# Two-layer streaming encoder: MLP evictions set between the squares at the layer's inner crossing, and the mixed queries of two attention heads kept on one bank

## The chip, the cores and the metric

One core of a Trainium2 chip runs the whole kernel in one launch. The metric is device time in microseconds, the median of several runs of the same program; lower is better.

## The reference, cut to what matters

The model is two layers on 560 tokens (512 frames, 16 meta tokens, 32 sample tokens), width 1024. Each layer mixes tokens in three branches, merges them, and ends in a squared-ReLU MLP:

```python
h = _rmsnorm(x, p['g_pre_mix'])
... = _split_cols(h @ p['w_in'])
oa = ...   # latent attention A, 8 heads, chunk-causal
x = x + _rmsnorm(mix, p['g_post_mix'])
f = jnp.square(jax.nn.relu(_rmsnorm(x, p['g_pre_mlp']) @ p['w_ff1'])) @ p['w_ff2']
return x + _rmsnorm(f, p['g_post_mlp'])
```

In latent attention each of 8 heads has 512 frame queries and 48 others: 16 meta queries, which see 16 meta keys, and 32 sample queries, which see 256 cached keys, 16 cached meta keys and 32 new keys. The 48 are the "mixed" queries of the change; they are scored against 320 keys under a mask:

```python
s_fr = jnp.where(visible, s_fr, NEG)
prob = jax.nn.softmax(jnp.concatenate([s_meta, s_fr], axis=-1), axis=-1).astype(v.dtype)
```

## The kernel before, in words

Tokens lie along the free dimension, in two halves of 280, and channels along the partitions. A dense projection is cut into units of 1024x128 weights. Each weight tile is loaded by SyncE into `wraw`, split by ScalarE into a rounded part `whi`, and by VectorE or GpSimd into the rest `wlo`. Each activation tile is split in the same way (`h_hi`, `h_lo`). For each of 8 k-tiles TensorE then does three matmuls (hi by hi, hi by lo, lo by hi) with 280 moving columns, so that a half unit ("half") is 24 matmuls, and a "pair" of units, interleaved by k-tile, is 48 (L926).

All engines walk one list of steps, `plan`, written out by hand in `lap` and `layer_plan`; each engine does its part of a step and skips the rest. So the order of steps in `plan` is the order on ScalarE and VectorE as well as on TensorE. Waits are on one counter for each engine.

`lap` writes the two crossings of a layer, where TensorE would otherwise wait for a norm: "post_mix" (from the output projection to `ff1`) and "post_mlp" (from `ff2` to the next layer). While TensorE does the last six units of the one projection on the second half of the tokens and the first six units of the next on the first half, VectorE and ScalarE bring the second half of `x` through two norms. For half 1 of "post_mix" the steps are: `rstd` of the first norm; for each pair of tiles j = 0 to 3, `norm` (VectorE L1820 and L1826: scale, add to x) and `square` (ScalarE L1416, then a sum on VectorE L1800); `sums`; a matmul with ones that sums over partitions (`mean_square`, step "ms", L940); `rstd` (ScalarE L1406 and L1407); `tokens`, which makes `h_raw` (L1854), `h_hi` (L1321) and `h_lo` (L1843). The evictions of the `ff1` units on half 0, three ScalarE instructions each (L1376 ReLU from PSUM, L1387 square, L1321 rounding), stand in the same list. `free` lets the planner put weight splits at that place, `hold` forbids it.

Latent attention has 16 jobs in a layer, (t, i): two heads t and 128 frame queries i. Step ("att", "a", j) does the scores of job j on TensorE, the transposes (`turn`) of job j-1 and the product with the values (`values`) of job j-2, and is followed by a dense unit. The jobs with i = 0, four in each layer, carry the mixed queries of both heads besides: scores of 48 queries by 320 keys for each head a, into banks S0 + a (L1140), softmax on VectorE, ScalarE and GpSimd over both heads as 48 partitions by 640 columns, and four transposes for each head (L1164).

Of the kernel before, what the change touches and what calls it, by code (L numbers as in the profile page):

```python
# [142 lines left out]
def build(nc, io, known):  # L143
    st = Steps(known)
    ctx = ExitStack()
    with ctx:
# [129 lines left out]
        ptm = at("ptm", [META, 2, 256], F32, work)  # L276
        stat, _ = wt("stat", [P, 2, 24])
# [35 lines left out]
        k_spread = sem("rope_keys_spread")  # L313
        state_loaded = sem("state_loaded")
# [68 lines left out]
        def program(block):  # L383
# [50 lines left out]
            def lap(l, post, pre, first, second):  # L434
# [36 lines left out]
                for i, u in enumerate(units[2:], 2):  # L471
                    if i == LAP - 3:
                        plan.append((l, ("hold",)))
# [245 lines left out]

            PARTS = (range(0, 4), range(4, 6), range(6, KD))  # L720
# [38 lines left out]
            def prob_view(j, i):  # L759
                nk = key_count("a", i)  # L760
                c0 = 2 * key_count("a", 0) if i == 4 else 0
                return prob[j % 2][:, c0:c0 + 2 * nk].rearrange("p (a n) -> p a n", a=2)

# [6 lines left out]
            def _(sp):  # L770
# [37 lines left out]
                for l, u in list(slot_of)[LAP:]:  # L808
# [29 lines left out]
            def _(pe):  # L838
# [277 lines left out]
                def scores(br, j):  # L1116
                    _, t, i = JOBS[br][j]
                    if br == "a":
# [10 lines left out]
                        for a in range(2):  # L1129
# [9 lines left out]
                            if i == 0:  # L1139
                                mm = pe.matmul(ps[0:MIXED, S0 + a, 144:144 + K_META], q_cat[:, h, META0:T], k_cat[:, h, 0:K_META],  # L1140
                                               start=False, stop=True, skip_group_check=True)
                    mm.then_inc(pe_done, st.done("pe", f"{br} scores {j}"))

                def turn(br, j):
# [8 lines left out]
                    if br == "a":  # L1153
                        for a in range(2):
# [5 lines left out]
                            if i == 0:  # L1160
                                pm = prob_view(j, 4)
                                idn = const[0:MIXED, 0:MIXED]
                                for n_, (c0, w) in enumerate(((0, 128), (128, 128), (CKEYS, MIXED), (PAST, META))):
                                    mm = pe.transpose(ps[0:w, T0 + a, 128 + 48 * n_:176 + 48 * n_], pm[0:MIXED, a, c0:c0 + w], idn)  # L1164
                    mm.then_inc(pe_done, st.done("pe", f"{br} turn {j}"))

                def values(j):
# [16 lines left out]
                    if i == 0:  # L1184
                        dst, mixed = ps[:, M_, 0:MIXED], slice(0, MIXED)
                        tiles = [(va_c[:, 0, :], lambda a: pt_third[:, a, 0:48], mixed), (va_c[:, 1, :], lambda a: pt_third[:, a, 48:96], mixed),
                                 (va_mix[:, :], lambda a: pt_third[0:MIXED, a, 96:144], mixed),
                                 (va_cm[:, :], lambda a: pt_third[64:64 + META, a, 144:192], mixed)]
# [115 lines left out]
            def _(act):  # L1304
# [281 lines left out]
                def att(br, j):  # L1586
                    n = len(JOBS[br])
                    if j < n:
                        _, t, i = JOBS[br][j]
                        k, sc = 2, A_SCALE  # L1590
                        for tile in tiles_of(br, i):
                            act.wait_ge(dve_done, A("dve", f"{br} shift {j} {tile}"))
                            pb = prob_view(j, tile)
                            w = pb.shape[2]
                            rows = P if tile < 4 else MIXED
                            s0 = 10 if br == "a" and tile == 4 else 8
# [87 lines left out]
            def _(dve):  # L1684
# [357 lines left out]
                def att(br, j, up):  # L2042

                    n = len(JOBS[br])
                    if j < n:
# [32 lines left out]
                        if br == "a" and i == 0:  # L2078
                            pb = prob_view(j, 4)
                            rows = MIXED  # L2080
                            sm = stat[0:rows, j % 2, :]
                            ms = c_("mask_s", MIXED).rearrange("p (a n) -> p a n", a=1).to_broadcast([MIXED, 2, 320])
                            link(dve.tensor_tensor(pb[0:rows, :, :], ps[0:rows, S0:S1 + 1, 144:464], ms, ALU.add), f"a shift {j}")
# [433 lines left out]
```

## Time and profile before

| what | value |
|---|---|
| median of 3 runs | 2343.1 us (2342.99 to 2345.57) |
| the profiled execution, its own time | 2343.32 us |
| its span | 2341.6 us |
| TensorE matmul busy | 2299.3 us, 98% |
| VectorE, ScalarE, GpSimd busy | 917.3, 997.4, 935.1 us |
| granted TensorE clock, mean | 0.997 |

The span is from the first to the last instruction on the core; 1.7 us of the execution's time lie around it. Matmuls are pipelined: the time from the start of one to the start of the next is what each one costs, and the durations shown overlap. A matmul of a full float32 operand has two records, one for each pass; a float32 transpose has one.

### The profile page before, as it was taken

The numbers are of one execution on the slowest core, as the hardware profiler recorded it, in microseconds if no ns is written. First come the engines' busy times: TensorE is split into PE (matmuls) and PEld (weight loads), VectorE is DVE, ScalarE is ACT, GpSimd is POOL, SyncE is SP. The second block draws the span as 40 slices with busy tenths as digits, with TensorE's granted clock in tenths as the row PEclk, the third lists the DMA queues.
The fourth block names the chain that finished last, engine by engine and source line by source line (L and its number), as shares of the span: only waits on it lengthen the run. The fifth ranks groups of instructions, "written<-read, shape, count | busy, mean of one in ns | idle before, by whom it ended". The sixth has DMA issues, their size and how long they took to land.

```text
span 2341.6 us, 41355 instructions
## 1 busy us (share of the span) xinstructions
PE 2299.3 (98%) x17536; PEld 2173.7 (93%) x17536; DVE 917.3 (39%) x1877; ACT 997.4 (43%) x1895; POOL 935.1 (40%) x598
## 2 busy tenths in 40 slices
PE   7999999999999999999999999999999999999997
PEld 7999978889899899999999999788999999999997
DVE  6566455543514401000575664555344152000014
ACT  4444334433555642432344444334345555423312
POOL 2222224344665354544412223144455644545532
PEclk9999999999999999999999999999999999999999
DMA  5122221112224122222321223211222241222222
GB/s 193 53 66 62 87 68 57 53 59 76 64 82 149 64 89 82 90 82 72 117 88 53 71 62 97 62 55 55 64 64 67 86 166 49 88 83 90 84 81 75
DMA packets 59368, 187.71 MB, mean 80 GB/s; under 512 B 8048, under 2 KB 17104, under 8 KB 58672
## 3 DMA queue, kind: packets, MB, share of 16 engines
q1 hardware_dynamic: 50960, 169.09, 22.7%
q10 hardware_dynamic: 8224, 15.97, 1.9%
q8 instruction: 140, 2.29, 0.4%
q14 instruction: 44, 0.36, 0.0%
HBM read 170.87 MB, written 10.89 MB: 78 GB/s over the span
## 4 chain that ended last, share of the span: by engine, by line
PE 92%; DVE 5%; ACT 2%; issue 1%; POOL 0%; DMA 0%; SPq 0%; DVEq 0%; ACTq 0%
PE dense L897 43%; PE att L897 30%; PE att L972 2%; PE att L1192 1%; PE att L1112 1%; PE att L1049 1%; PE dense L926 1%; PE att L1132 1%; PE att L1230 1%; PE att L1053 1%; PE att L1035 1%; PE att L1156 1%; PE att L1265 1%; PE att L1136 1%; PE att L926 1%
## 5 line engine op out<-in xcount | busy, mean ns | idle before, releaser
L2243 POOL TENSOR_TENSOR wlo<-wraw,whi 128x1024 fp32r<-128x1024 f32 x245 | 587.8, 2406 | 592.4 <-ACT whi L1317 592.4
L897 PE MATMUL dense<-h_hi,whi 128*128 128x280 f32 x1888 | 556.6, 295 | 1.2 <-ACT hid_raw L1376 0.9
L897 PE MATMUL dense<-h_lo,whi 128*128 128x280 f32 x1888 | 550.4, 292 | 0.0
L897 PE MATMUL dense<-h_hi,wlo 128*128 128x280 f32 x1888 | 549.3, 291 | 0.0
L1317 ACT ACTIVATE whi<-wraw 128x1024 fp32r<-128x1024 f32 x302 | 314.8, 1050 | 268.4 <-DMA wraw<-in_w 266.6
L897 PEld LDWEIGHTS dense<-h_hi,whi 128*128 128x128 f32 x1888 | 355.0, 188 | 14.6 <-issue 9.4
L897 PEld LDWEIGHTS dense<-h_hi,wlo 128*128 128x128 f32 x1888 | 354.5, 188 | 0.5
L897 PEld LDWEIGHTS dense<-h_lo,whi 128*128 128x128 f32 x1888 | 354.8, 188 | 0.0
L897 PE MATMUL att<-h_hi,whi 128*128 128x280 f32 x1024 | 299.3, 292 | 0.4 <-issue 0.4
L897 PE MATMUL att<-h_lo,whi 128*128 128x280 f32 x1024 | 298.4, 291 | 0.0
L897 PE MATMUL att<-h_hi,wlo 128*128 128x280 f32 x1024 | 297.8, 291 | 0.0
L897 PE MATMUL att<-hid_hi,whi 128*128 128x280 f32 x672 | 196.0, 292 | 0.0
L897 PEld LDWEIGHTS att<-h_hi,whi 128*128 128x128 f32 x1024 | 192.4, 188 | 3.5 <-ACT sig L1340 1.6
L897 PE MATMUL att<-hid_lo,whi 128*128 128x280 f32 x672 | 195.7, 291 | 0.0
L897 PE MATMUL att<-hid_hi,wlo 128*128 128x280 f32 x672 | 195.4, 291 | 0.0
L897 PEld LDWEIGHTS att<-h_hi,wlo 128*128 128x128 f32 x1024 | 192.3, 188 | 0.3
L897 PEld LDWEIGHTS att<-h_lo,whi 128*128 128x128 f32 x1024 | 192.4, 188 | 0.0
L2248 POOL TENSOR_TENSOR hid_lo<-hid_raw,hid_hi 128x560 fp32r<-128x560 f32 (+1 forms) x76 | 91.5, 1204 | 246.5 <-ACT hid_hi L1321 246.5
L2291 POOL TENSOR_TENSOR level<-bcum 128x256 f32<-128x256 f32 (+2 forms) x56 | 40.4, 722 | 262.8 <-DVE bcum L1875 262.8
L897 PEld LDWEIGHTS att<-hid_hi,whi 128*128 128x128 f32 x672 | 126.3, 188 | 0.1
L897 PEld LDWEIGHTS att<-hid_lo,whi 128*128 128x128 f32 x672 | 126.3, 188 | 0.0
L897 PEld LDWEIGHTS att<-hid_hi,wlo 128*128 128x128 f32 x672 | 126.2, 188 | 0.1
(361 smaller groups left out, 4624.4 us busy)
## 6 DMA issues: line engine op xcount, KB each, us to landing
wraw<-in_w SPq DMA_DIRECT2D x302, 512.0 KB, 3.5
x_spill<-x ACTq DMA_DIRECT2D x2, 2240.0 KB, 6.9
x<-x_spill ACTq DMA_DIRECT2D x2, 2240.0 KB, 12.3
k_cat<-k_rope SPq DMA_DIRECT2D x16, 212.0 KB, 3.4
x<-in_x SPq DMA_DIRECT2D x4, 560.0 KB, 6.0
out_y_out<-x SPq DMA_DIRECT2D x4, 560.0 KB, 3.1
out_c_out<-ckv SPq DMA_DIRECT2D x2, 560.0 KB, 5.3
state<-in_state ACTq DMA_DIRECT2D x8, 128.0 KB, 2.1
```

The costliest lines, as they stand in the source:

```text
L897: mm = pe.matmul(bank(u, o, hf)[0:m, :], a[:, k, o * 128:o * 128 + m], b[:, k, H[hf]], start=(k == 0 and i == 0), stop=(k == kt - 1 and i ...
L926: mm = pe.matmul(bank(u, 0, hf)[0:m, :], a[:, k, 0:m], b[:, k, H[hf]], start=(k == 0 and i == 0), stop=(k == KD - 1 and i == 2))
L972: mm = pe.matmul(ps[0:rows, PAIR_BANK[i], c0:c0 + 64].rearrange("p (g t) -> p g t", t=m), e[:, 128 * sb:128 * sb + rows], late, start=(n_ ...
L1035: mm = pe.matmul(ps[:, bank, 256 * (sb % 2):256 * (sb % 2) + 256], ktok[0:n, sb, :], vtok[0:n, sb, :], start=(sb % 2 == 0), stop=True, ski ...
L1049: pe.matmul(dst, vtok[0:n, sb, 128 * vt:128 * vt + 128], amat[0:n, a:a + n], start=first, stop=(sb == 0), skip_group_check=True)
L1053: mm = pe.matmul(dst, state[:, STATE_IN[sb], 128 * vt:128 * vt + 128], qe[:, a:a + n], start=False, stop=True, skip_group_check=True)
L1112: mm = pe.matmul(ps[0:n, pair + i, 0:512], src[:, k, a:a + n], wuv[:, k, :], start=(k == 0), stop=(k == KL - 1))
L1132: mm = pe.matmul(ps[:, S0 + a, 0:META + 128 * (i + 1)], q_cat[:, h, 128 * i:128 * i + 128], k_cat[:, h, K_META:K_FRAME + 128 * (i + 1)], s ...
L1317: act.activation(whi[slot][:, :], wraw[slot][:, :], ACT.Copy).then_inc(act_done, st.done("act", f"w hi {u}"))
L2243: pool.tensor_tensor(wlo[slot][:, :], wraw[slot][:, :], whi[slot][:, :].bitcast(F32), ALU.subtract).then_inc(pool_done, st.done("pool", f" ...
L2248: pool.tensor_tensor(lo, raw, hi.bitcast(F32), ALU.subtract).then_inc(pool_done, st.done("pool", name))
L2291: pool.tensor_tensor(e_first, ref, b_first, ALU.subtract).then_inc(pool_done, st.done("pool"))
```

## The change

Two things are changed.

At the "post_mix" crossing the steps of half 1 are written in another order: the pair of the first two `ff1` units and its evictions come ahead of the second square, the third unit's half comes ahead of the third square and the fourth unit's ahead of the last. TensorE's own order is the same as before.

In the attention jobs with i = 0 the mixed queries of head 0 are given 64 columns (48, and 16 columns of the next head that nothing reads) and those of head 1 48 columns, on output partitions 0 to 63 and 64 to 111 of the one bank S0. From there on both heads are one tile of 112 partitions by 320 columns: two mask additions, one reduction, one subtraction, one exponential, one reciprocal, one multiplication, and four transposes of 112 rows in place of eight of 48. The second head's mask is a new tile, `mixed_mask`, on partitions 64 to 111, which SyncE loads in each layer behind the weights of unit up_c 1, after it has waited for the outputs that lay there (`latent_stored`).

```diff
+        mixed_mask = at("mixed_mask", [P, 320], F32, work)
...
-                crossed(1, 1)
-                plan.append((l1, ("pair", units[0:2], 0, (l, post))))
-                crossed(1, 2)
-                crossed(1, 3)
-                plan.extend([(l, ("sums", pre, 1)), (l, ("free",))])
-                plan.extend([(l1, ("after", v, 0)) for v in units[0:2]])
+                if post == "post_mix":
+                    plan.append((l1, ("pair", units[0:2], 0, (l, post))))
+                    plan.extend([(l1, ("after", v, 0)) for v in units[0:2]])
+                    plan.append((l, ("hold",)))
+                    crossed(1, 1)
+                    plan.append((l1, ("half", units[2], 0)))
+                    crossed(1, 2)
+                    plan.append((l1, ("half", units[3], 0)))
+                    crossed(1, 3)
+                    plan.extend([(l, ("sums", pre, 1)), (l, ("free",)), (l, ("hold",))])
+                else:
...
+                    if UNITS[u] == ("up_c", 1):
+                        sp.wait_ge(latent_stored, 32 * (l + 1))
+                        sp.wait_ge(pe_done, A("pe", f"gla z {C_HEADS - 1}", l))
+                        m0 = CONST["mask_s"][0]
+                        sp.dma_start(mixed_mask[64:64 + MIXED, :], io["const"][0:MIXED, m0:m0 + 320]).then_inc(mask_loaded, 16)
...
-                            if i == 0:
-                                mm = pe.matmul(ps[0:MIXED, S0 + a, 144:144 + K_META], q_cat[:, h, META0:T], k_cat[:, h, 0:K_META],
-                                               start=False, stop=True, skip_group_check=True)
+                        if i == 0:
+                            every_q = q_cat.rearrange("p h t -> p (h t)")
+                            for a, n in ((0, 64), (1, MIXED)):
+                                h = 2 * t + a
+                                mm = pe.matmul(ps[64 * a:64 * a + n, S0, 144:144 + K_META], every_q[:, h * T + META0:h * T + META0 + n],
+                                               k_cat[:, h, 0:K_META], start=False, stop=True, skip_group_check=True)
...
-                                for n_, (c0, w) in enumerate(((0, 128), (128, 128), (CKEYS, MIXED), (PAST, META))):
-                                    mm = pe.transpose(ps[0:w, T0 + a, 128 + 48 * n_:176 + 48 * n_], pm[0:MIXED, a, c0:c0 + w], idn)
+                                n = 128 + TWO_MIXED
+                                for bank_, c0, at_c, w in ((T0, 0, 128, 128), (T0, 128, n, 128), (T1, CKEYS, 128, MIXED), (T1, PAST, n, META))[2 * a:2 * a + 2]:
+                                    mm = pe.transpose(ps[0:w, bank_, at_c:at_c + TWO_MIXED], prob_mixed(j)[:, c0:c0 + w],
+                                                      const[0:TWO_MIXED, 0:TWO_MIXED])
...
+                            dve.wait_ge(mask_loaded, 16 * (l + 1))
+                            both = ps[0:rows, S0, 144:464]
+                            dve.tensor_tensor(pb[0:64, :], both[0:64, :], c_("mask_s", 64), ALU.add).then_inc(dve_done, st.done("dve"))
+                            link(dve.tensor_tensor(pb[64:rows, :], both[64:rows, :], mixed_mask[64:rows, :], ALU.add), f"a shift {j}")
+                            link(dve.tensor_reduce(sm[:, 6:7], pb[:, :], AX.X, ALU.max))
+                            dve.tensor_tensor(pb[:, :], pb[:, :], sm[:, 6:7].to_broadcast([rows, 320]), ALU.subtract
```

Line numbers of the changed kernel are higher by 31 or more at the places shown below (L1416 is L1447 in it, L1376 is L1407, L1132 is L1157).

ScalarE at the "post_mix" crossing of layer 0, before; `nsum<-x` are the squares, `hid_raw` and `hid_hi` the evictions of `ff1` units, `whi` a weight split:

```order
546 L1317 ACTIVATE whi_80<-wraw_54 128x1024
547 L1317 ACTIVATE whi_81<-wraw_55 128x1024
548 L1416 ACTIVATE nsum<-x 128x560 x4
549 L1317 ACTIVATE whi_82<-wraw_56 128x1024
550 L1376 ACTIVATE hid_raw<-dense 128x280
551 L1387 ACTIVATE hid_raw<-hid_raw 128x280
552 L1321 ACTIVATE hid_hi<-hid_raw 128x280
553 L1376 ACTIVATE hid_raw<-att 128x280
554 L1387 ACTIVATE hid_raw<-hid_raw 128x280
555 L1321 ACTIVATE hid_hi<-hid_raw 128x280
```

All four squares stand ahead of the first eviction. The same place in the changed kernel, from the first square to the last:

```order
548 L1447 ACTIVATE nsum<-x 128x560
549 L1407 ACTIVATE hid_raw<-dense 128x280
550 L1418 ACTIVATE hid_raw<-hid_raw 128x280
551 L1352 ACTIVATE hid_hi<-hid_raw 128x280
552 L1407 ACTIVATE hid_raw<-att 128x280
553 L1418 ACTIVATE hid_raw<-hid_raw 128x280
554 L1352 ACTIVATE hid_hi<-hid_raw 128x280
555 L1447 ACTIVATE nsum<-x 128x560
556 L1407 ACTIVATE hid_raw<-att 128x280
557 L1418 ACTIVATE hid_raw<-hid_raw 128x280
558 L1352 ACTIVATE hid_hi<-hid_raw 128x280
559 L1447 ACTIVATE nsum<-x 128x560
```

Two evictions now stand behind the first square, one behind the second and, in the rows that follow, one behind the third; `whi_82` comes behind the fourth square as before, and only the fifth unit's eviction is left behind the second `rstd`, where it was before too. VectorE's order at the crossing does not change.

TensorE at the transposes of the first job with i = 0 (layer 0), before; `const` is the identity:

```order
1937 L1156 MATMUL att<-const,prob_142 128x128
1938 L1158 MATMUL att<-const,prob_142 16x128
1939 L1164 MATMUL att<-const,prob_142 128x48 x2
1940 L1164 MATMUL att<-const,prob_142 48x48
1941 L1164 MATMUL att<-const,prob_142 16x48
1942 L1156 MATMUL att<-const,prob_142 128x128
1943 L1158 MATMUL att<-const,prob_142 16x128
1944 L1164 MATMUL att<-const,prob_142 128x48 x2
1945 L1164 MATMUL att<-const,prob_142 48x48
1946 L1164 MATMUL att<-const,prob_142 16x48
```

and in the changed kernel:

```order
1936 L1184 MATMUL att<-const,prob_142 128x128
1937 L1186 MATMUL att<-const,prob_142 16x128
1938 L1191 MATMUL att<-const,prob_142 128x112 x2
1939 L1184 MATMUL att<-const,prob_142 128x128
1940 L1186 MATMUL att<-const,prob_142 16x128
1941 L1191 MATMUL att<-const,prob_142 48x112
1942 L1191 MATMUL att<-const,prob_142 16x112
```

Twelve transposes have become eight. TensorE at the scores of the same job, in the changed kernel, with a row of the dense units on either side (before, the order was frames, mixed, frames, mixed):

```order
1883 L922 MATMUL dense<-oc_lo,whi_77 128x280
1884 L1157 MATMUL att<-k_cat,q_cat 128x144 x2
1885 L1168 MATMUL att<-k_cat,q_cat 64x320
1886 L1168 MATMUL att<-k_cat,q_cat 48x320
1887 L922 MATMUL dense<-h_hi,whi_75 128x280
```

The two mixed matmuls now stand side by side.

## Rows read from the trace of the kernel before

**Rows 1.** The page: busy time, share and instructions of each engine.
```profile
PE 2299.3 (98%) x17536; PEld 2173.7 (93%) x17536; DVE 917.3 (39%) x1877; ACT 997.4 (43%) x1895; POOL 935.1 (40%) x598
```

**Rows 2.** Waits of TensorE: waiter, releaser, total us, times, longest.
```profile
PE dense L926 <- DVE h_lo L1843: 7.7, 4, 3.4
```

**Rows 3.** Timeline, TensorE, crossing of layer 0: start, us, instruction, idle before.
```profile
783.56 0.74 PE L940 MATMUL att<-nsum,const 128*128 128x280 f32 x2 [0.44 <-DVE nsum L1803]
784.74 0.37 PE L897 MATMUL dense<-h_hi,whi 128*128 128x280 f32 x1 [0.45 <-ACT hid_raw L1376]
...
787.78 0.29 PE L897 MATMUL dense<-h_lo,whi 128*128 128x280 f32 x1
791.50 0.37 PE L926 MATMUL dense<-h_hi,whi 128*128 128x280 f32 x1 [3.43 <-DVE h_lo L1843]
...
799.43 0.29 PE L897 MATMUL att<-h_hi,whi 128*128 128x280 f32 x1
```

**Rows 4.** Stretches of TensorE: length, busy (matmuls), granted clock, DMA share, GB/s.
```profile
792.98:796.39 3.41, 3.41 (x16) 0.50 0.00 0
796.39:799.43 3.04, 3.04 (x25) 1.00 0.02 5
```

**Rows 5.** Timeline, ScalarE, the same crossing.
```profile
777.28 0.67 ACT L1416 ACTIVATE nsum<-x 128x560 f32<-128x560 f32 x1 [3.27 <-DVE x L1826]
...
781.57 0.67 ACT L1416 ACTIVATE nsum<-x 128x560 f32<-128x560 f32 x1 [1.47 <-DVE x L1826]
...
783.10 0.38 ACT L1376 ACTIVATE hid_raw<-dense 128x280 f32<-128x280 f32 x1
...
788.02 0.48 ACT L1406 ACTIVATE rstd<-att,const 128x280 f32<-128x280 f32 x1
```

**Rows 6.** Timeline, VectorE, the same crossing.
```profile
794.39 1.38 DVE L1843 TENSOR_TENSOR h_lo<-h_raw,h_hi 128x560 fp32r<-128x560 f32 x2
```

**Rows 7.** Timeline, TensorE, scores of an i = 0 job (its second).
```profile
387.64 0.41 PE L1132 MATMUL att<-k_cat,q_cat 128*128 128x144 f32 x2
387.98 0.74 PE L1140 MATMUL att<-k_cat,q_cat 128*48 128x320 f32 x2
388.65 0.51 PE L1132 MATMUL att<-k_cat,q_cat 128*128 128x144 f32 x2
389.09 0.74 PE L1140 MATMUL att<-k_cat,q_cat 128*48 128x320 f32 x2
389.76 0.66 PE L1156 MATMUL att<-const,prob 128*128 128x128 f32 x4
```

**Rows 8.** Timeline, TensorE, transposes of the same job, to the next matmul.
```profile
397.98 0.27 PE L1156 MATMUL att<-const,prob 128*128 128x128 f32 x1
...
398.29 0.40 PE L1164 MATMUL att<-const,prob 48*128 48x48 f32 x4
...
399.33 0.65 PE L1192 MATMUL att<-ptf,va 128*64 128x256 f32 x3
```

**Rows 9.** Timeline, TensorE, transposes of an i = 1 job, six in all.
```profile
409.20 0.38 PE L1156 MATMUL att<-const,prob 128*128 128x128 f32 x2
...
409.95 0.44 PE L1192 MATMUL att<-pt_third,va_c 128*64 128x48 f32 x8
```

**Rows 10.** Timeline, TensorE, values of branch B: two outputs, partitions 0-63 and 64-127, one bank.
```profile
588.68 0.59 PE L1265 MATMUL att<-ptf,v_own 128*64 128x512 f32 x1
588.68 0.59 PE L1265 MATMUL att<-ptf_second,v_own 128*64 128x512 f32 x1
589.11 0.59 PE L1265 MATMUL att<-ptf,v_prev 80*64 80x512 f32 x1
```

**Rows 11.** Timeline, GpSimd: the softmax multiplications of the i = 0 job.
```profile
395.24 1.87 POOL L2316 TENSOR_TENSOR prob<-prob,stat 128x288 f32<-128x288 f32 x2 [5.01 <-DVE stat L2134]
```

**Rows 12.** Timeline, SyncE's queue, from unit gate_c 1 on: start, us to the last issue.
```profile
316.45 1.04 SPq L823 DMA_DIRECT2D out_kr_out<-kra  x1
330.86 20.41 SPq L779 DMA_DIRECT2D wraw<-in_w  x2
```

More of the change, by code:

```diff
@@ L464, in lap @@
                 plan.extend([(l, ("rstd", post, 1)), (l, ("norm", post, 1, 0)), (l, ("free",)), (l, ("square", pre, 1, 0))])
-                crossed(1, 1)
-                plan.append((l1, ("pair", units[0:2], 0, (l, post))))
-                crossed(1, 2)
-                crossed(1, 3)
-                plan.extend([(l, ("sums", pre, 1)), (l, ("free",))])
-                plan.extend([(l1, ("after", v, 0)) for v in units[0:2]])
+                if post == "post_mix":
[9 more added lines that the diff above has]
+                else:
+                    crossed(1, 1)
+                    plan.append((l1, ("pair", units[0:2], 0, (l, post))))
+                    crossed(1, 2)
+                    crossed(1, 3)
+                    plan.extend([(l, ("sums", pre, 1)), (l, ("free",))])
+                    plan.extend([(l1, ("after", v, 0)) for v in units[0:2]])
                 for i, u in enumerate(units[2:], 2):
+                    if post == "post_mix" and i < 4:
+                        continue
                     if i == LAP - 3:
@@ L1185, in values, with of_head @@
                         dst, mixed = ps[:, M_, 0:MIXED], slice(0, MIXED)
-                        tiles = [(va_c[:, 0, :], lambda a: pt_third[:, a, 0:48], mixed), (va_c[:, 1, :], lambda a: pt_third[:, a, 48:96], mixed),
-                                 (va_mix[:, :], lambda a: pt_third[0:MIXED, a, 96:144], mixed),
-                                 (va_cm[:, :], lambda a: pt_third[64:64 + META, a, 144:192], mixed)]
+                        turned = pt_third.rearrange("p a n -> p (a n)")
+                        def of_head(rows, n):
+                            return lambda a: turned[rows, TWO_MIXED * n + 64 * a:TWO_MIXED * n + 64 * a + MIXED]
+                        tiles = [(va_c[:, 0, :], of_head(slice(0, P), 0), mixed), (va_c[:, 1, :], of_head(slice(0, P), 1), mixed),
+                                 (va_mix[:, :], of_head(slice(0, MIXED), 2), mixed), (va_cm[:, :], of_head(slice(64, 64 + META), 3), mixed)]
                     for n_, (v, pt, cols) in enumerate(tiles):
@@ L1592, in att @@
                             act.wait_ge(dve_done, A("dve", f"{br} shift {j} {tile}"))
+                            if tile == 4:
+                                act.activation(prob_mixed(j), prob_mixed(j), ACT.Exp, scale=sc, accum_out=stat[0:TWO_MIXED, j % 2, 10:11]
+                                               ).then_inc(act_done, st.done("act", f"{br} exp {j} {tile}"))
+                                continue
                             pb = prob_view(j, tile)
                             w = pb.shape[2]
-                            rows = P if tile < 4 else MIXED
-                            s0 = 10 if br == "a" and tile == 4 else 8
+                            rows, s0 = P, 8
                             for a in range(k):
@@ L2126, in att @@
                     if j < n:
-                        k = 2
                         i = JOBS[br][j][2]
                         for tile in tiles_of(br, i):
-                            s0 = 2 if br == "a" and tile == 4 else 0
-                            sm = stat[0:P if tile < 4 else MIXED, j % 2, :]
+                            s0, k = (2, 1) if tile == 4 else (0, 2)
+                            sm = stat[0:P if tile < 4 else TWO_MIXED, j % 2, :]
                             dve.wait_ge(act_done, A("act", f"{br} exp {j} {tile}"))
@@ L2310, in att @@
                             pool.wait_ge(dve_done, A("dve", f"{br} rsum {j} {tile}"))
[L2311 to L2316 removed]
+                            if tile == 4:
+                                pb = prob_mixed(j)
+                                rs = stat[0:TWO_MIXED, j % 2, 14:15].to_broadcast([TWO_MIXED, 320])
+                            else:
+                                pb = prob_view(j, tile)
+                                rs = stat[:, j % 2, 12:14].rearrange("p (a n) -> p a n", n=1).to_broadcast([P, k, pb.shape[2]])
+                            pool.tensor_tensor(pb, pb, rs, ALU.mult
                                                ).then_inc(pool_done, st.done("pool", f"{br} prob {j}" if tile == tiles_of(br, i)[-1] else None))
```

30 lines of the change are left out of this document (12 added, 18 removed).

## The prediction

> **What bounds the kernel now.** I read the page's busy times first: TensorE's matmuls fill 98% of the span and no other engine passes 43% [rows 1]. So a change is worth what it takes out of TensorE's row of instructions, idle time or issue time, and work saved on VectorE, ScalarE and GpSimd counts only where TensorE waits for it. The list of TensorE's waits comes next. The largest entry inside the kernel, 7.7 us in four waits, is a matmul of a pair (L926) that waits for `h_lo`; the longest is 3.4 us [rows 2]. The timeline puts one at 791.50 in layer 0 [rows 3]; layer 1 has its twin, and the other two of the four are 0.4 us each. The 791.50 matmul is the first of the pair on half 1, behind the norm that crosses from the output projection into the MLP. Then the granted clock: 1.5 us after the pair starts it falls to 0.50 for 3.41 us, the lower of its two levels (1.2 of 2.4 GHz), and TensorE gets 16 matmuls done in 3.41 us where it did 25 in the 3.04 us that followed [rows 4]. What the engine did before the fall was to stand idle for 3.43 us; after the waits of 0.4 us in the same stretch it did not fall. I charge the fall to the long wait. From the last matmul ahead of the wait, 787.78, to the first behind the pair, 799.43, 11.65 us pass [rows 3] for 48 matmuls.
>
> **Why the pair waits.** The chain is: sum of squares, matmul with ones at 783.56 [rows 3], `rstd` on ScalarE, `h_raw`, `h_hi`, `h_lo`, pair. The matmul with ones is over at 784.30 (783.56 and 0.74), but `rstd` starts at 788.02 [rows 5]. In between ScalarE does four evictions of `ff1` units, from 783.10 to 788.02, 1.23 us each. So the chain is held 3.7 us by evictions that could have been done earlier: ScalarE had idled 3.27 us ahead of the square at 777.28 and 1.47 us ahead of the one at 781.57 [rows 5].
>
> **The change, part by part. 1: the crossing.** Of those four evictions two go behind the first square, one behind the second, one behind the third. Do they fit without making a square late? TensorE does units back to back ahead of the matmul with ones, so its ends follow backwards from 783.56 - 0.44 = 783.12 [rows 3] in steps of 24 x 0.128 = 3.07 us: 780.05 for the fourth unit, 776.98 for the third, 773.9 for the pair. The first two evictions are ready at 773.9; 2 x 1.23 us bring ScalarE to 776.4, before x is ready for the square at 777.28. That square ends at 777.95, and the third eviction, whose unit is done by then, ends at 779.2, ahead of the third square, which comes 2.15 us after the second (the four are evenly spaced from 777.28 to 781.57 [rows 5]). The third square ends at 780.1, the fourth eviction at 781.4, and the last square comes at 781.57. The margins are 0.9, 0.2 and 0.2 us: thin, but a miss costs only its own amount. So the sum, and the matmul with ones, stay at 783.56, and `rstd` starts at 784.34 (in this crossing ScalarE starts 0.04 us after that matmul ends): 3.68 us earlier. All behind it moves by as much; the fifth eviction keeps its place behind `rstd`. The pair could start at 791.50 - 3.68 = 787.82, and TensorE is free at 787.78 + 0.13 = 787.91. The wait is gone, and with it, I take it, the slow clock.
>
> After it the pair needs `h_lo` at full speed. The third of its `lo` instructions, which with the fourth starts at 794.39 and takes half of 1.38 us [rows 6], ends at 791.4 when moved, and its k-tile is wanted at 791.2 (787.99 and four k-tiles of 6 x 0.128 us). I book 0.4 us for such small waits. The pair then takes 0.13 + 0.08 + 48 x 0.128 + 0.4 = 6.75 us in place of 11.65: 4.9 us. Layer 1's stretch is 0.1 us shorter, so 4.8. **Sum 9.7 us**; bounds: 10.6 without the small waits, and nothing if the squares are pushed so far that the old wait returns.
>
> **2: scores of the mixed queries.** Eight jobs in the two layers have them. Now such a job's scores take 389.76 - 387.64 = 2.12 us: for each head two frame passes of 144 columns and two mixed ones of 320. A mixed pair of passes costs 0.67 us (387.98 to 388.65) [rows 7], against 0.53 at the rate of two columns a cycle that 512 columns in 0.43 us show [rows 10]; the rest, with 0.1 us more on the frame pass ahead and 0.1 on the one behind, is the price of going from 128 output columns to 48 and back, paid twice. In the changed order the four frame passes stand together, 3 x 0.12 + 0.22, and the two mixed matmuls write partitions 0 to 63 and 64 to 111 of one bank. The trace has that form in branch B: two matmuls on halves of one bank start at the same time (588.68 both) and the next two come 0.43 us later, the time of one [rows 10]. So both heads cost what one does, 0.67. Sum 1.25, saving 0.87 us a job, **7.0 us in all**. The lower bound is that the two do not run together: 0.61 more a job, which leaves 2.1 us.
>
> **3: transposes.** Now 399.33 - 397.98 = 1.35 us for twelve [rows 8], where six of an i = 1 job, all on 128 rows, take 0.75: 0.11 each and 0.09 for the change to the 64-wide values behind them [rows 9]. A mixed group of four is cheap by its columns, but from the start of the first at 398.29 back to the next head's 128-row transpose takes 0.33 us and the way in another 0.09: the array is switched to a smaller row group and back for each head. With 112 rows I expect no switch, since matmuls on 80 rows followed those on 128 after the plain 0.43 us [rows 10]. Then eight take 4 x 0.11 + 4 x 0.096 + 0.09 = 0.91 us: 0.44 saved a job, **3.5 us in all**. If 112 rows did switch, four changes at 0.09 would leave 0.1 a job, 0.6 us.
>
> **4: the other engines.** On VectorE the mask, the reduction and the subtraction of a mixed tile fall from 640 columns to 320 (the mask in two instructions); ScalarE saves one exponential, GpSimd half of its second multiplication. None is on TensorE's path: the multiplications of job 4 end at 395.24 + 1.87 = 397.11 [rows 11], 0.87 us ahead of the transposes at 397.98 that wait for them. They get shorter, so I book nothing; what counts is that the shorter scores do not make GpSimd late, and the shorter softmax covers that. The job before loses 0.87 us of its lead (it has 1.8 us).
>
> **5: the mask's load.** SyncE now waits, behind the load of up_c 1, for `kr_out`'s landing. That store is issued at 316.45, and the load of up_c 1 is not issued before 330.86 [rows 12], when it has long landed; the mask is wanted past 353, at the first job's softmax, and is 61 KB. Booked at nothing, with some 20 us of cover.
>
> **The sum.** 9.7 + 7.0 + 3.5 = 20.2 us off the profiled execution's 2343.3, which is 0.2 above the median of 2343.1. So 2343.1 - 20.2 = **2322.9 us**.
>
> **The rivals.** (a) *The two mixed matmuls go one after the other* (chance 0.14). For it: these are 64 and 48 columns wide, not 64 and 64, and of float32 passes; against it, the pairs of rows 10. The gain is 9.7 + 2.1 + 3.5 = 15.3 us: 2327.8. The Trainium skill's page "TensorEngine Tiling (Array Packing)", under Gotcha 1: PSUM Pressure, says that different row tiles cannot access the same PSUM bank at the same time. By that rule, if it held for these two tiles, the kernel would come out at rival (a)'s time; the trace's pairs in one bank are tiles side by side in columns, and they do run together.
> (b) *112 rows are a form of their own* (0.07): 17.3 us gained, 2325.8.
> (c) *The crossing keeps its wait* (0.10). The margins of 0.2 us ahead of the third and fourth squares are eaten, or a dip of the clock stays although the wait is short. If all is kept, 10.5 us are gained: 2332.6; if half is, 2327.7.
> (d) *Slower* (0.03): the mask's load holds SyncE's queue, and with it the weight loads behind it. The next load is issued 20.4 us behind that of up_c 1 [rows 12], so a hold decides only from 20 + 10 us on in each layer (past the slack, TensorE would have to lose over 10.1 us, twice, to eat the 20.2): at 32 us, 2347. The trace speaks against it, since `kr_out` has 14 us to land before the wait is even reached.
> (e) *The change at the crossing and the concurrency as forecast, or with losses of some tenths a job in attention* (0.66): 2322.9, own range 2320.5 to 2326.
>
> **How the numbers follow.** The likeliest is (e), 2322.9. Upwards the range must take in (a), (b) and half of (c), to 2329.5; what is left out above is the full (c) and (d), about 0.1. Downwards the bound is no small waits in the pairs and transposes at the price of their columns, some 2 us more: 2320. What a measurement of this kernel can tell from no change is 0.2%, 4.7 us; every case but (d) gains more than that. Chances: faster 0.95, same 0.02, slower 0.03.
>
> **What would show it.** Part 1: no idle time ahead of the first matmul of the half-1 pair and no stretch at clock 0.50 before the end; `rstd` within 0.1 us of the end of the matmul with ones; 6.7 us from 48 matmuls. It is wrong if the squares start later against TensorE's units or the fall of the clock remains. Part 2: both mixed matmuls of a pass start within 0.01 us, and the block takes 1.25 us; if it takes 1.9, rival (a). Part 3: a block of 0.9 us; if 1.25, rival (b). Part 5: SyncE's loads at the same distance from the units.

## The result, and the profile after

The changed kernel takes 2327.1 us (median of four runs, 2326.3 to 2328.8); the kernel before, timed on the same chip, takes 2344.3. The ratio is 0.9926 with an interval of 0.9914 to 0.9938: 17.2 us faster by the medians, 16.3 by the spans of the two profiled executions (2341.6 and 2325.3). The forecast was 2322.9, a gain of 20.2; the measured time lies in the range of 2320 to 2329.5, 4.2 us above the likeliest value and above that case's own range of 2320.5 to 2326. The gain by the medians is only 3.0 us short, because the median of the kernel before has itself moved from 2343.1 to 2344.3; between the profiled executions it is 3.9 short, and that is what is explained below.

The page, where [rows 1] stood for the kernel before:

```profile
PE 2287.0 (98%) x17504; PEld 2170.0 (93%) x17504; DVE 917.2 (39%) x1885; ACT 996.0 (43%) x1879; POOL 933.9 (40%) x598
```

TensorE still sets the time. Its waits (waiter, releaser, total us, times, longest), against [rows 2]:

```profile
PE att L965 <- DVE nsum L1837: 15.4, 5, 10.9
...
PE dense L951 <- DVE h_lo L1877: 0.8, 2, 0.4
```

The wait of the pair for `h_lo` has lost its two long members: 7.7 us have become 0.8. But the first line has grown: the matmul with ones (L965, L940 before) waits for `nsum`. The same line of the list of before was

```profile
PE att L940 <- DVE nsum L1803: 12.3, 5, 10.8
```

The longest of the five is at the kernel's start in both. Of the 3.1 us more, 3.0 are in the two crossings. The timeline of TensorE at the crossing of layer 0, and behind the "..." one row of layer 1 at its end, against [rows 3]:

```profile
777.73 0.29 PE L922 MATMUL att<-h_lo,whi 128*128 128x280 f32 x1
779.96 0.74 PE L965 MATMUL att<-nsum,const 128*128 128x280 f32 x2 [1.94 <-DVE nsum L1837]
781.14 0.37 PE L922 MATMUL dense<-h_hi,whi 128*128 128x280 f32 x1 [0.44 <-issue]
...
784.20 0.29 PE L922 MATMUL dense<-h_lo,whi 128*128 128x280 f32 x1
784.32 0.31 PE L951 MATMUL dense<-h_hi,whi 128*128 128x280 f32 x1
...
791.21 0.29 PE L922 MATMUL att<-h_hi,whi 128*128 128x280 f32 x1
...
1929.69 1.30 PE L965 MATMUL att<-nsum,const 128*128 128x280 f32 x2 [1.93 <-DVE nsum L1837]
```

The pair (784.32) starts without idle time, as forecast. The matmul with ones, which had waited 0.44 us, waits 1.94. From the last matmul ahead of it, 777.73, to the first behind the pair, 791.21, are 13.48 us; the same stretch was 16.60 us before. In layer 1 it is 14.02 in place of 16.46. I call this the crossing's stretch from here on; its gain is 3.12 + 2.44 = 5.56 us, where 9.7 were forecast.

ScalarE at the same crossing, against [rows 5]:

```profile
775.28 0.68 ACT L1447 ACTIVATE nsum<-x 128x560 f32<-128x560 f32 x1 [0.24 <-DVE x L1860]
...
780.74 0.49 ACT L1437 ACTIVATE rstd<-att,const 128x280 f32<-128x280 f32 x1 [1.14 <-PE att L965]
```

The third square still finds ScalarE idle and waits 0.24 us for VectorE's `x`, and the fourth waits 0.79: the evictions fit into ScalarE, as worked out. `rstd` starts 0.04 us after the matmul with ones is over (779.96 + 0.74 = 780.70). What is late is `x`. VectorE, from the first multiplication behind the first square on (L1854 is the multiplication by `rstd`, in two instructions that are one row here, L1860 the sum into `x`):

```profile
770.39 1.46 DVE L1854 SCALAR_TENSOR_TENSOR mix<-mix,par,rstd 128x280 f32<-128x280 f32 x2
771.95 1.15 DVE L1860 TENSOR_TENSOR x<-x,mix 128x560 f32<-128x560 f32 x1
773.02 0.92 DVE L1854 SCALAR_TENSOR_TENSOR mix<-mix,par,rstd 128x280 f32<-128x280 f32 x2
...
775.17 1.47 DVE L1854 SCALAR_TENSOR_TENSOR mix<-mix,par,rstd 128x280 f32<-128x280 f32 x2
...
777.22 0.73 DVE L1860 TENSOR_TENSOR x<-x,mix 128x560 f32<-128x560 f32 x1
```

Two of the three multiplication pairs take 1.46 and 1.47 us where the middle one takes 0.92, and the first sum takes 1.15 where the last takes 0.73. The excess is 0.54 + 0.42 + 0.55 = 1.51 us, just what the matmul with ones waits longer (1.94 less 0.44). GpSimd in the same stretch:

```profile
770.23 0.89 POOL L2284 TENSOR_TENSOR hid_lo<-hid_raw,hid_hi 128x280 fp32r<-128x280 f32 x1 [27.38 <-ACT hid_hi L1352]
771.46 1.04 POOL L2284 TENSOR_TENSOR hid_lo<-hid_raw,hid_hi 128x280 fp32r<-128x280 f32 x1 [0.34 <-ACT hid_hi L1352]
775.12 0.79 POOL L2284 TENSOR_TENSOR hid_lo<-hid_raw,hid_hi 128x280 fp32r<-128x280 f32 x1 [2.62 <-ACT hid_hi L1352]
777.27 1.31 POOL L2284 TENSOR_TENSOR hid_lo<-hid_raw,hid_hi 128x280 fp32r<-128x280 f32 x1 [1.36 <-ACT hid_hi L1352]
```

Its subtractions follow each eviction (`hid_lo` is `hid_raw` less `hid_hi`), so they moved with the evictions. At 770.23, 771.46 and 775.12 they lie on the three slow steps of VectorE, and the fast one, 773.02, has none beside it. The fourth subtraction, at 777.27, shows that the order matters: VectorE's sum had begun 0.05 us earlier, at 777.22, and kept its 0.73 us, and it is the subtraction that takes 1.31 us instead of 0.79. The three slow steps of VectorE each began after the subtraction beside them. Here the one that starts second pays, and roughly what is left of the first: the sum at 771.95 began 0.55 us before the subtraction of 771.46 ended (772.50), and took 0.42 us more.

The granted clock, against [rows 4]:

```profile
1929.67:1933.08 3.41, 3.39 (x11) 0.50 0.01 2
...
780.00:783.40 3.40, 2.96 (x19) 1.00 0.00 0
```

The clock did not fall in layer 0 (1.00 behind a wait of 1.94 us), but it did in layer 1, for the same 3.41 us as before, behind a wait of 1.93 us. The prediction had named a fall that remains as a sign of being wrong.

The attention of the job of [rows 7] and [rows 8], first scores, then transposes:

```profile
386.37 0.65 PE L1157 MATMUL att<-k_cat,q_cat 128*128 128x144 f32 x4
386.95 0.75 PE L1168 MATMUL att<-k_cat,q_cat 128*64 128x320 f32 x4
387.63 0.33 PE L1184 MATMUL att<-const,prob 128*128 128x128 f32 x1
...
395.85 0.27 PE L1184 MATMUL att<-const,prob 128*128 128x128 f32 x1
396.07 0.36 PE L1191 MATMUL att<-const,prob 112*128 112x112 f32 x2
...
396.77 0.44 PE L1223 MATMUL att<-ptf,va 128*64 128x256 f32 x2
```

Scores are 387.63 - 386.37 = 1.26 us (1.25 forecast), transposes 396.77 - 395.85 = 0.92 (0.91 forecast). Summed over all jobs of both layers the score blocks went from 51.62 to 44.80 us and the transpose blocks from 33.33 to 29.55: 6.8 and 3.8, in place of 7.0 and 3.5. With the crossing's 5.6 that is 16.2 us, and the spans differ by 16.3. Nothing else of weight is in the difference.

### The profile page after: what moved, and what is told of

Same layout as the page of the kernel before. It is cut to its first block, busy times and chain, and to the rows that moved or that the text cites. A ratio compares the mean times of both kernels' runs of the same rounds, so it can differ in the third digit from the quotient of the medians.

```text
span 2325.3 us, 41287 instructions
## 1 busy us (share of the span) xinstructions
PE 2287.0 (98%) x17504; PEld 2170.0 (93%) x17504; DVE 917.2 (39%) x1885; ACT 996.0 (43%) x1879; POOL 933.9 (40%) x598
## 4 chain that ended last, share of the span: by engine, by line
PE 92%; DVE 5%; ACT 2%; issue 1%; POOL 0%; DMA 0%; SPq 0%; DVEq 0%; ACTq 0%
PE dense L922 43%; PE att L922 30%; PE att L997 2%; PE att L1223 1%; PE att L1137 1%; PE att L1074 1%; PE att L1157 1%; PE att L1261 1%; PE att L1078 1%; PE dense L951 1%; PE att L1060 1%; PE att L1296 1%; PE att L1184 1%; PE att L1161 1%; DVE x L1860 1%
```

## The experiments

The theory: *the crossing's missing 4 us come from GpSimd's subtractions, which moved with the evictions and slow VectorE's three steps ahead of the last square.* Rivals: the evictions themselves do it on ScalarE; GpSimd being busy at all does it, whatever it runs; or the shortfall lies where the two parts of the change meet.

### Each part alone

The crossing's order alone, with attention as before:

```diff
 (before, and in lap():)
+                if post == "post_mix":
+                    plan.append((l1, ("pair", units[0:2], 0, (l, post))))
+                    plan.extend([(l1, ("after", v, 0)) for v in units[0:2]])
...
```

> The kernel before with the new order at the crossing alone. Theory (the two parts add up, and GpSimd's early hid_lo subtractions hold VectorE): 5.6 us off, 0.9976 of before, and the matmul with ones waits 1.9 us as in the changed kernel. Rival (the shortfall of the changed kernel comes from the two parts together): the crossing alone gives the 9.7 us that were forecast for it, 0.9959, with a wait of 0.44 us.

Measured: 2338.9 us against 2344.6, ratio 0.9976 (0.9966 to 0.9986), span 2337.1, 4.5 us less than before. The medians give the 5.6 us that the theory expected. The matmul with ones waits 1.93 and 1.92 us, the stretches are 14.17 and 14.26 us, and the clock fell at both crossings.

Attention alone, with the old order at the crossing:

```diff
 (after, and in lap(), for post_mix too:)
+                crossed(1, 1)
+                plan.append((l1, ("pair", units[0:2], 0, (l, post))))
+                crossed(1, 2)
+                crossed(1, 3)
```

> The changed kernel with the old order at the crossing. Theory: 10.6 us off, 0.9955 of before, and at both crossings the wait of 3.4 us ahead of the pair and a fall of the clock for 3.41 us behind it. Rival (shorter attention steps make something else late): clearly under 10 us, with new waits of TensorE among the attention steps.

Measured: 2332.7 us, ratio 0.9949 (0.9934 to 0.9964), span 2330.3. The pair waits 3.43 and 3.45 us as before, the clock falls at both crossings, and no other wait is new. The spans differ by 11.3 us where 10.6 were expected. 5.7 and 11.9 us from the parts make 17.6, against 17.2 for both: the parts add up, so the shortfall is the crossing's own and is there with the old attention too.

### Moving GpSimd's subtractions away

The changed kernel with one wait more on GpSimd: the half-0 subtractions of the first six `ff1` units start only when VectorE has done its last sum into `x`.

```diff
+ if u in V_MLP and hfs == (0,):
+     pool.wait_ge(dve_done, A("dve", "x post_mix 7 1"))
```

> The changed kernel, but GpSimd begins the hid_lo subtractions of the first six ff1 units on half 0 only when VectorE has added the last tiles to x. ScalarE's evictions stay where they are. Theory (GpSimd's reads hold VectorE's two-input instructions): the three slow VectorE steps (1.46, 1.15 and 1.47 us) go back to 0.92, 0.74 and 0.92, x is ready 1.5 us earlier; the last sums and the h_raw and h_lo behind it now meet GpSimd's four subtractions and lose up to half of it again. 1 to 3 us less than the changed kernel, 0.9914 to 0.9922 of before. Rival (ScalarE's evictions hold VectorE, or the instructions are slow for their place): the three steps stay slow and the time is that of the changed kernel, 0.9926.

Measured: 2326.7 us, ratio 0.9924 (0.9911 to 0.9936), span 2324.1: hardly less than the changed kernel, and just outside what was expected. The three steps are fast again (0.93, 0.74 and 0.92 us), so the first half of the theory held. But the subtractions now run in one block behind them, and it meets the next steps of the chain. VectorE, then GpSimd, of this kernel:

```profile
777.85 0.91 DVE L1837 TENSOR_TENSOR nsum<-nsum 128x280 f32<-128x280 f32 x1
778.68 1.79 DVE L1726 TENSOR_TENSOR wlo<-wraw,whi 128x1024 fp32r<-128x1024 f32 x1
```

```profile
776.42 4.70 POOL L2284 TENSOR_TENSOR hid_lo<-hid_raw,hid_hi 128x280 fp32r<-128x280 f32 x4 [33.67 <-DVE x L1860]
```

The last addition of the squares takes 0.91 us (0.45 before) and the weight subtraction ahead of `h_raw` 1.79 (1.22 before). The matmul with ones waits 0.90 us instead of 1.94. The first matmul of the next unit then waits 1.02 us instead of 0.44; the view puts this down to ScalarE, but in the profiles of all twelve kernels of this case, in both layers, that matmul starts 0.10 us after VectorE's weight subtraction ends (here 778.68 + 1.79 = 780.47, and the matmul at 780.58), so the longer subtraction is the cause. The stretches are 12.69 us in layer 0 and 13.83 in layer 1, where the clock fell behind these two waits:

```profile
1927.71 0.50 PE L965 MATMUL att<-nsum,const 128*128 128x280 f32 x1 [0.90 <-DVE nsum L1837]
...
1929.60:1933.00 3.40, 3.40 (x15) 0.50 0.00 0
```

So the wait was put in the wrong place. The next kernel puts it behind the last `lo` of the crossing, where VectorE has nothing left that TensorE waits for:

```diff
+ if u in V_MLP and hfs == (0,):
+     pool.wait_ge(dve_done, A("dve", "pre_mlp lo 7 1"))
```

> As e3_low_after_x, but GpSimd waits until VectorE has made the last h_lo of half 1. Theory: no GpSimd work beside the chain at all; the matmul with ones waits 0.44 us, the stretch from the last matmul of the fifth unit to the first behind the pair goes from 13.5 and 14.0 us to about 11.7 in both layers, the clock does not fall at either crossing: 4 us less than the changed kernel, about 2323, 0.991 of before, if GpSimd's delayed work makes no weight split late. Rival: as the changed kernel, 0.9926.

Measured: 2324.0 us (2323.0 to 2324.4), ratio 0.9911 (0.9897 to 0.9924), span 2322.3. TensorE and VectorE of this kernel:

```profile
779.75 0.74 PE L965 MATMUL att<-nsum,const 128*128 128x280 f32 x2 [0.44 <-DVE nsum L1837]
```

```profile
771.66 0.93 DVE L1854 SCALAR_TENSOR_TENSOR mix<-mix,par,rstd 128x280 f32<-128x280 f32 x2
772.69 0.74 DVE L1860 TENSOR_TENSOR x<-x,mix 128x560 f32<-128x560 f32 x1
...
775.50 0.93 DVE L1854 SCALAR_TENSOR_TENSOR mix<-mix,par,rstd 128x280 f32<-128x280 f32 x2
```

The matmul with ones waits 0.44 us, VectorE's steps are at their old length, the clock falls at neither crossing, and the stretches are 11.59 and 11.60 us: 5.0 and 4.9 us less than before, where 4.9 and 4.8 had been forecast for the change. ScalarE's evictions stand where the changed kernel has them, so they are not the cause.

### GpSimd work added to the kernel before

The mirror image: the kernel before, whose evictions stand behind the squares, with two subtractions of 128x280 added on GpSimd behind each of the first three sums into `x`. ScalarE's order is untouched.

```diff
+ elif step[0] == "norm" and step[1:3] == ("post_mix", 1) and step[3] in (1, 2, 3):
+     pool.wait_ge(dve_done, A("dve", f"x post_mix {2 * step[3] - 1} 1"))
+     for _ in range(2):
+         pool.tensor_tensor(sig[:, 1, H[0]], sig[:, 0, H[0]], sig[:, 0, H[1]], ALU.subtract)
```

> The kernel before, in which GpSimd does two subtractions of 128x280 on a tile that nothing reads (an eighth of a busy us each is not the point, they are 0.8 us each) whenever VectorE has finished one of the first three additions to x at the half-1 crossing. ScalarE's order is untouched: no eviction stands among the squares. Theory (GpSimd's reads hold VectorE): the VectorE steps that meet them take 0.4 to 0.55 us more each, the matmul with ones comes 1 to 3 us later, its wait grows by as much, and the pair's start too: 2 to 6 us slower than before, 1.001 to 1.0025. Rival (it was ScalarE's evictions): VectorE's steps keep 0.92 and 0.74 us and the time stays.

The same with three fills of 128x560 in place of the two subtractions: GpSimd busy at the same places, but reading nothing.

```diff
+     for _ in range(3):
+         pool.memset(sig[:, 1, :], 0.0)
```

> The same, with three memsets of 128x560 in place of the two subtractions, 0.57 us each: GpSimd writes but reads nothing. If it is the reads of GpSimd that VectorE's two-input instructions wait for, they keep 0.92 and 0.74 us and the time is that of before. If any work of GpSimd slows them, the steps grow as in e5_added_gpsimd.

Measured: with the subtractions 2349.8 us, ratio 1.0021 (1.0012 to 1.0031), and the matmul with ones waits 3.88 and 3.86 us, 3.4 more than before and a little over the 1 to 3 expected; with the fills 2345.1, ratio 1.0003 (0.9994 to 1.0013), and it waits 0.45 in both layers. VectorE and GpSimd with the subtractions:

```profile
779.13 0.74 DVE L1826 TENSOR_TENSOR x<-x,mix 128x560 f32<-128x560 f32 x1
779.79 1.47 DVE L1820 SCALAR_TENSOR_TENSOR mix<-mix,par,rstd 128x280 f32<-128x280 f32 x2
781.18 1.34 DVE L1800 TENSOR_TENSOR nsum<-nsum 128x560 f32<-128x560 f32 x1
...
780.02 1.91 POOL L2343 TENSOR_TENSOR sig<-sig 128x280 f32<-128x280 f32 x2 [1.72 <-DVE x L1826]
```

and with the fills:

```profile
778.78 0.93 DVE L1820 SCALAR_TENSOR_TENSOR mix<-mix,par,rstd 128x280 f32<-128x280 f32 x2
779.62 0.73 DVE L1800 TENSOR_TENSOR nsum<-nsum 128x560 f32<-128x560 f32 x1
...
778.98 1.82 POOL L2343 MEMSET sig<- 128x560 f32 x3 [2.20 <-DVE x L1826]
```

With a subtraction beside it a pair takes 1.47 us instead of 0.93 and a sum 1.34 instead of 0.73; the sum at 779.13, which has none beside it, keeps its 0.74. With 1.82 us of fills beside them the same steps keep 0.93 and 0.73. So it is GpSimd's subtractions, and not GpSimd being busy or writing, that hold VectorE; what the fills lack is the reading. The Trainium skill, "SBUF — State Buffer", section "Who interferes with whom", says that a VectorE instruction with two inputs in SBUF shares its second input's way with GpSimd's reads, and that a GpSimd instruction that only writes does not disturb it. These two kernels agree with that.

### Where the attention gain comes from

The kernel before with its matmuls in another order only: frames of both heads, then the mixed queries of both heads, still on 48 partitions of two banks.

```diff
-                            if i == 0:
-                                mm = pe.matmul(ps[0:MIXED, S0 + a, ...
+                        if i == 0:
+                            for a in range(2):
+                                mm = pe.matmul(ps[0:MIXED, S0 + a, ...
```

> The kernel before, with the scores of an i = 0 job in the order frames of both heads, then mixed of both heads; both mixed matmuls still write partitions 0 to 47, in two banks, so they cannot run side by side. The theory of the prediction prices this at 1.86 us a block against 2.12 before and 1.26 in the changed kernel: 0.26 us of the 0.86 come from the switches that are no longer paid twice, 0.60 from the two heads running at once. Rival (grouping alone does it, or the one bank does): a block of about 1.26 us.

One run: 2341.1 us, span 2339.4; what counts here is the block, in the job of [rows 7], and it is the same in all eight:

```profile
387.88 0.65 PE L1132 MATMUL att<-k_cat,q_cat 128*128 128x144 f32 x4
388.46 1.28 PE L1142 MATMUL att<-k_cat,q_cat 128*48 128x320 f32 x4
389.67 0.66 PE L1158 MATMUL att<-const,prob 128*128 128x128 f32 x4
```

The block takes 1.79 us (1.86 expected), between 2.12 before and 1.26 after. Of the 0.86 us that a job saves, 0.33 is one round of switching between 128 and 48 output columns, and 0.53 is the two heads running at once: four mixed passes take 389.67 - 388.46 = 1.21 us here and 387.63 - 386.95 = 0.68 in the changed kernel. Here the four start one behind the other, at 388.46, 388.77, 389.04 and 389.31; in the changed kernel they start in pairs, one of each head, at 386.95 and 386.96 and at 387.26 and 387.27.

Likewise for the transposes, first the four of 128 rows, then the eight of 48:

```diff
-                            if i == 0:
-                                pm = prob_view(j, 4)
+                        if i == 0:
+                            pm = prob_view(j, 4)
+                            for a in range(2):
```

> The kernel before, with the transposes of an i = 0 job in the order: the four on 128 rows of both heads, then the eight on 48 rows. If the price is a switch of the array to a smaller row group and back, paid for each head, one of two round trips goes: about 0.2 us less than 1.35, so 1.15 us a block. If the eight small transposes cost by themselves (the other reading), the block stays at 1.35 us.

One run: 2342.7 us, span 2341.0; the block:

```profile
398.18 0.27 PE L1156 MATMUL att<-const,prob 128*128 128x128 f32 x1
...
398.70 0.62 PE L1165 MATMUL att<-const,prob 48*128 48x48 f32 x8
399.25 0.65 PE L1193 MATMUL att<-ptf,va 128*64 128x256 f32 x4
```

It takes 1.07 us instead of 1.35 (1.15 expected), so one way into 48 rows and back costs 0.28 us. What the second costs shows best in the first job of each layer, where a dense matmul on 128 by 128 follows: there the block takes 1.35 us before, 1.07 here and 0.76 in the changed kernel. In the other six jobs the changed kernel's block takes 0.92 us, where matmuls with 64 output columns follow.

The Trainium skill, "TensorEngine Tiling (Array Packing)", section Key Properties, says that a change of tiling drains TensorE and that different tiles run in parallel. The trace shows the second in the starts 0.01 us apart. Of the first it shows the price of a change, 0.28 to 0.33 us for a round, but not that it is a drain.

### Once more, and the better version

Both the changed kernel and the one with the later subtractions, again on one chip, to bound what separates them and to see whether the clock falls in the same places.

> The changed kernel once more, beside e10 on one chip: 0.9926 of before. By the theory its time moves between runs by 1.7 us steps, with the number of crossings (0, 1 or 2) at which the clock falls.

> The kernel of e4_low_after_tokens once more, beside the changed kernel on one chip: 0.991 of before and 3 to 4 us under the changed kernel; less than 2 us would mean that e4's advantage was that of its chip.

Measured: the changed kernel 2328.9 us (2326.7 to 2329.1), ratio 0.9929 (0.9916 to 0.9943); with the later subtractions 2323.8 (2322.9 to 2324.0), ratio 0.9910 (0.9896 to 0.9923). The second is 5.1 us faster on this chip, and its stretches are 11.60 and 11.58 us again without a fall. In the changed kernel the clock now fell at both crossings, behind waits of 1.93 and 1.91 us, and the stretches are 14.15 and 14.11 us. The 1.7 us steps that were expected are not there: with the fall the stretch of layer 0 is only 0.67 us longer than the 13.48 of the first profiled execution. The window of the fall in layer 0:

```profile
781.98:785.39 3.41, 3.06 (x13) 0.50 0.00 0
```

## Why the prediction was 4 us off

**The bound and the shape of the gain: right.** TensorE's row was what counted. All three terms came, and the spans' difference is their sum. But the likeliest case missed by more than its own range allowed, and the stated range held the result only because it had been widened upwards for rivals (a) and (c), neither of whose mechanisms is what happened. That it held is partly luck.

**Part 1, the crossing, 9.7 us: the term that was mis-sized; it gave 5.6.** The failed step is the sentence "So the sum, and the matmul with ones, stay at 783.56": the wait of that matmul went from 0.44 to 1.94 us. The steps around it held: the evictions fit between the squares on ScalarE, `rstd` started 0.04 us behind the matmul with ones, and the pair had no idle time ahead of it. What I checked was whether the evictions fit on ScalarE. I didn't follow them to GpSimd, which does a subtraction for each, nor look at what VectorE does at that time. The missing 4.3 us, against the kernel in which the forecast came true (stretches of 11.59 and 11.60), split so:

- 2 x 1.5 us: the matmul with ones is late by the three slowed steps of VectorE.
- 0.4 us in layer 0: from the last matmul ahead of the pair, 784.20, to the pair's end, 791.21, are 7.02 us in place of 6.65. This is GpSimd again: its subtraction for the fifth unit (783.01) holds the first `h_lo` (783.30), which takes 0.82 us against 0.45 in that kernel. TensorE is then late at two k-tiles, 786.12 and 788.04, by 0.5 us together and 0.08 more for each restart; I had booked 0.4 us for one.
- 0.9 us in layer 1: the fall of the clock behind the new wait, 11 matmul records in 3.41 us, less what it hides of such small waits.

"The wait is gone, and with it, I take it, the slow clock" held in layer 0 only, and its premise, that the long wait brings the fall, is weaker than I took it: in the kernel with the fills, layer 1, the pair waits 3.42 us and no fall follows. That stretch is 15.62 us against 16.46 before, so a fall there is worth 0.84 us and most of the forecast 4.9 is the wait itself.

That the slowing comes from GpSimd's subtractions is shown from both sides: taken away from those steps the loss is gone, and added to the kernel before it appears. The trace of before had it on show, at the same crossing, in rows that I hadn't read. VectorE, then GpSimd, there:

```profile
790.55 0.80 DVE L1843 TENSOR_TENSOR h_lo<-h_raw,h_hi 128x280 fp32r<-128x280 f32 x1 [0.20 <-ACT h_hi L1321]
...
791.69 0.43 DVE L1843 TENSOR_TENSOR h_lo<-h_raw,h_hi 128x280 fp32r<-128x280 f32 x1
...
790.27 0.77 POOL L2248 TENSOR_TENSOR hid_lo<-hid_raw,hid_hi 128x280 fp32r<-128x280 f32 x1 [1.30 <-ACT hid_hi L1321]
```

The same instruction on the same shape takes 0.80 us beside GpSimd's subtraction, which had begun 0.28 us earlier, and 0.43 alone.

**Part 2, scores, 7.0: 6.8.** The two mixed matmuls run at once in one bank, and rival (a) is out: the block takes 1.26 us, not 1.9. **Part 3, transposes, 3.5: 3.8.** 112 rows are no form of their own, and rival (b) is out: 0.92 us, not 1.25. Six jobs save 0.43 us each, as forecast; the 0.3 us more come from the first job of each layer, which saves 0.59, since I had priced all eight by one that is followed by 64-wide values.

**Part 4, other engines at nothing: right.** No new wait of TensorE came from the softmax. **Part 5, the mask's load at nothing: right.** SyncE's queue after the change, with the load of up_c 1, the mask and the next weight load:

```profile
331.03 0.33 SPq L799 DMA_DIRECT2D wraw<-in_w  x1
331.46 0.38 SPq L848 DMA_DIRECT2D mixed_mask<-in_const  x1
351.13 0.33 SPq L799 DMA_DIRECT2D wraw<-in_w  x1
```

The mask goes out 0.43 us behind the load ahead of it, and the next load comes 20.1 us after that one, as before (the 20.4 us of the prediction include the last issue's own 0.3).

**Slips that moved nothing.** The squares evenly spaced from 777.28 to 781.57 are the last three, not four; the first is at 773.36. The k-tile in question was wanted at 787.99 + 3.07 = 791.06, not 791.2. The bound without small waits is 9.7 + 0.8 = 10.5 us, not 10.6. And 512 columns in 0.43 us at 2.4 GHz are two cycles a column, not "two columns a cycle"; the price of 0.53 us is worked out from the columns and the time and stands.

**The rivals.** Rival (c) gave the nearest time, 2327.7 "if half is" kept (rival (a) gave 2327.8, so the time alone could not have told them apart), and the dip of the clock that it feared is part of the loss. But its mechanism isn't what happened: the margins on ScalarE were not eaten, and the old wait is gone. It took a third engine to make the squares late. The chance of 0.10 was low for a step whose margins were called thin.

## What to carry to other kernels

When an instruction moves, list everything that follows it on other engines and moves along, and look at what the third engine does in the place where it arrives: a free slot on the engine of the edit isn't a free slot on the chip. Ahead of a chain that TensorE waits for, keep GpSimd's reading instructions off VectorE's steps with two inputs, or at least from starting just ahead of them; here a step that met one already running cost 0.4 to 0.6 us, and holding back work that is wanted later took one wait and gave 3 to 5 us. Search the trace of before for one instruction of the same shape with two durations: the difference is the price of a collision, and what lies beside the longer one is the first suspect.

## What the hardware showed unexpectedly

- GpSimd is slowed as well: a subtraction of 128x280 takes 0.79 us alone and up to 1.31 when a step of VectorE with two inputs had begun just before it.
- The clock fell for 3.41 us behind some waits and not behind others alike: in the changed kernel behind 1.93 us in layer 1 and not behind 1.94 us in layer 0, and in its second profiled execution at both places; with the first delay of GpSimd, behind waits of 0.90 and 1.02 us in layer 1 and not behind the same two in layer 0; with the fills, behind 3.43 us in layer 0 and not behind 3.42 us in layer 1; never where no wait at the crossing was over 0.45 us. What decides between them stays open. In layer 0 of the changed kernel a fall makes the stretch 0.67 us longer (14.15 against 13.48), much less than the 1.7 us that 3.41 us at half clock would lose: the slower TensorE is no longer late for `h_lo`, and the pair's part of the stretch is 6.32 us against 7.02.
- Two profiled executions of the same kernel differ by 1.2 us ahead of the crossing (the matmul with ones starts at 779.96 and at 781.15), so here the stretches say more than single profiled times.
